# Four pieces of a hybrid decoder layer's schedule are moved: the level 1 update, the third level mask, the relative bias products, the second solution

## The reference

```python
y_s5 = s5_mixer(...)        # z = gelu(y); z * sigmoid(z @ w_glu + b_glu); y from a complex scan over time
y_rw = rwkv7_mixer(...)     # state = state*w + sa*kka + v*k, one step per token
y_mb = moba_mixer(p_mb, rel_bias)   # s = q.k + bias_t[:, t5_bucket(rel)]
y = rms_norm(y.reshape(..., N_GROUPS, GW), mix_out_gain)   # one norm per group
return y.reshape(..., D_MIX) @ w_out
```

## Time and profile before

| | us |
|---|---|
| median of 3 runs | 527.93 |
| lowest and highest | 526.81, 528.66 |
| the profiled execution | 526.82 |
| its span, first to last instruction | 525.0 |
| TensorE busy | 489.0 (93%) |
| VectorE busy | 378.7 (72%) |
| ACT busy | 261.2 (50%) |
| POOL busy | 172.1 (33%) |

### The profile page before, as it was taken

The page is one execution under the profiler, slowest core; times in us unless marked ns, Lnnn a source line. Parts: engine busy times, 40 slices in busy tenths (PEclk is TensorE's granted clock), DMA queues, the critical chain, the costliest instruction groups (busy, mean ns, idle before and its releaser), DMA issues.

```text
span 525.0 us, 8449 instructions
## 1 busy us (share of the span) xinstructions
PE 489.0 (93%) x3478; PEld 447.8 (85%) x3478; DVE 378.7 (72%) x443; ACT 261.2 (50%) x410; POOL 172.1 (33%) x103
## 2 busy tenths in 40 slices
PE   0799999889999999999999995999999999999986
PEld 0789989788898888878999884999999999988874
DVE  5675897997766987679655457589999999962114
ACT  3598774331633244657945547454444443443333
POOL 0030317397669250000000001254433443353440
PEclk9999999989999999999999997899999999999999
DMA  8837328022041023535545241356445555545602
GB/s 345 365 96 248 120 93 308 1 81 81 9 153 53 31 81 116 205 99 223 191 171 201 80 150 40 132 199 236 168 161 168 196 198 180 205 161 196 222 0 81
DMA packets 12358, 79.33 MB, mean 151 GB/s; under 512 B 1440, under 2 KB 2080, under 8 KB 3488
## 3 DMA queue, kind: packets, MB, share of 16 engines
q1 hardware_dynamic: 12320, 78.79, 42.3%
HBM read 76.95 MB, written 1.84 MB: 150 GB/s over the span
## 4 chain that ended last, share of the span: by engine, by line
PE 83%; DVE 9%; ACT 3%; issue 2%; DMA 1%; POOLq 0%; POOL 0%; SPq 0%; DVEq 0%; ACTq 0%
PE bank L369 81%; DMA ring<-weights 1%; DVE arena L1635 1%; DVE vx L1662 1%; ACT w_high L344 1%; DVE arena L1452 1%; PE bank L857 1%; POOLq L89 0%; POOL w_rest L350 0%; DVE arena L1627 0%; DVE we_rest L350 0%; DVE arena L1628 0%; DVE wk_rest L350 0%; DVE arena L1806 0%; DVE wm_rest L350 0%
## 5 line engine op out<-in xcount | busy, mean ns | idle before, releaser
L344 ACT ACTIVATE w_high<-ring 128x1024 fp32r<-128x1024 f32 x70 | 73.6, 1058 | 79.7 <-PE bank L369 79.7
L369 PE MATMUL bank<-h_high,w_high 128*128 128x256 f32 x384 | 103.0, 284 | 0.0
L369 PE MATMUL bank<-h_rest,w_high 128*128 128x256 f32 x352 | 99.7, 283 | 0.0
L369 PE MATMUL bank<-h_high,w_rest 128*128 128x256 f32 x320 | 90.7, 283 | 0.0
L350 DVE TENSOR_TENSOR w_rest<-ring,w_high 128x1024 fp32r<-128x1024 f32 x42 | 53.5, 1279 | 44.2 <-ACT w_high L344 44.1
L350 POOL TENSOR_TENSOR w_rest<-third_slot,w_high 128x1024 fp32r<-128x1024 f32 x11 | 26.5, 2407 | 161.4 <-ACT w_high L344 161.4
L350 POOL TENSOR_TENSOR w_rest<-ring,w_high 128x1024 fp32r<-128x1024 f32 x22 | 53.6, 2438 | 74.8 <-ACT w_high L344 74.8
L369 PEld LDWEIGHTS bank<-h_high,w_high 128*128 128x128 f32 x384 | 71.7, 192 | 0.5 <-issue 0.4
L369 PEld LDWEIGHTS bank<-h_rest,w_high 128*128 128x128 f32 x352 | 67.6, 192 | 0.0
L369 PE MATMUL bank<-arena 128*128 128x128 f32 (+7 forms) x496 | 59.4, 300 | 6.5 <-DVE arena L1658 4.5
L369 PEld LDWEIGHTS bank<-arena 128*128 128x128 f32 (+3 forms) x496 | 52.9, 183 | 12.6 <-DVE arena L1658 5.1
(11 more groups left out here) (308 smaller groups left out, 1227.2 us busy)
## 6 DMA issues: line engine op xcount, KB each, us to landing
ring<-weights SPq DMA_DIRECT2D x50, 1024.0 KB, 4.9
third_slot<-weights SPq DMA_DIRECT2D x15, 1024.0 KB, 4.9
cst<-consts SPq DMA_DIRECT2D x1, 1664.0 KB, 12.3
gain<-gains SPq DMA_DIRECT2D x3, 512.0 KB, 5.9
par<-params SPq DMA_DIRECT2D x1, 1168.0 KB, 14.6
kx<-x_t SPq DMA_DIRECT2D x1, 1024.0 KB, 4.9
vx<-mem_t SPq DMA_DIRECT2D x1, 1024.0 KB, 10.3
xres<-x_rows SPq DMA_DIRECT2D x1, 1024.0 KB, 10.5
```

Source lines behind the costliest of these rows:

```text
L344: nc.scalar.activation(split_half(i)[0], raw_half(i), ACT.Copy).then_inc(S["w_high"], 1)
L369: return nc.tensor.matmul(out_, lhsT, rhs, start=start, stop=stop, skip_group_check=True)
```

## The change

- On TensorE the four bias products stand behind `x_sumsq`, ahead of all projections. They wait for a new semaphore, `onehot_in`; the waits for the large constants and parameters move to the product rw_w.
- The one-hot table moves to the front of the large constants and is loaded by a DMA of its own, 33 partitions of 384, between slots 0 and 1. Only those 33 rows are loaded; before, all 128 were.
- On VectorE, `level_update(1)` and one of the two rests ahead of it stand before `scan(0)`, the other rest between the update and the scan.
- On POOL, `level_mask(3)` stands before `rotate_back(0)`.
- On VectorE, `solution(1)` and one rest stand ahead of the first `sigmoid_of_exp` of S5.
- On TensorE, `gn_s5` stands after step 1 of the output product instead of step 0.

No instruction is added or removed but the one DMA. Some lines of the changed kernel are numbered one to three apart from before.

```diff
--- before.py
+++ after.py
@@ -43,11 +43,10 @@
 
 
 CONST, NCONST = columns([
-    ("ones", P), ("eps6", 1), ("eps12", 1), ("eps_gn", 1), ("eps6_xd", 1), ("round", 1), ("half_pi", 1), ("ident", P), ("pair_ones", P), ("strict", P), ("incl", P), ("causal_add", 384),
+    ("ones", P), ("eps6", 1), ("eps12", 1), ("eps_gn", 1), ("eps6_xd", 1), ("round", 1), ("half_pi", 1), ("onehot", 384), ("ident", P), ("pair_ones", P), ("strict", P), ("incl", P), ("causal_add", 384),
     ("levels", LEVELS * P), ("level0_t", P), ("time", T), ("head_sel", NH * P), ("pair_sel", 2 * P),
-    ("onehot", 384),
 ])
-CONST_FIRST = CONST["ident"][0]
+CONST_FIRST, CONST_MORE = CONST["onehot"]
 
 PARAM, NPARAM = columns([
     ("mu", 8), ("w0", 2), ("a0", 2), ("k_k", 2), ("k_a", 2), ("r_k", 2), ("ln_w", 2), ("ln_b", 2),
@@ -254,7 +253,7 @@
             ml_log ml_cur ml_conv ml_silu ml_E mb_max mb_exp rw_rstd s5_arg s5_exp rw_out s5_out post_sq post_root
             post_part pre_part pre_sq pre_root gain_pre_in x_max f_exp rw_kx rw_G0 rw_k2 s5_co_step
             ml_row_step ml_den mb_inv s5_step2 rw_tail s5_sig x_inv f_sig s5_sq s5_root ml_sq
-            ml_root rw_sq rw_root mb_sq mb_root
+            ml_root rw_sq rw_root mb_sq mb_root onehot_in
             w_high w_rest_even w_rest_odd w_rest_mid w_used high_ready act_rest y_rest h_high h_rest x_summed
             mem_summed
             """.split()}
@@ -566,13 +565,12 @@
             o = pe_open(pe, "x_sumsq", 0)
             pe.wait_ge(S["x_summed"], 4)
             mm(o[:, 0:T], const("ones"), sq_x[:, 0, :]).then_inc(full[0], 1)
-            split_channel_major(0, "rw_wag", 1, h_split, lambda j: pe.wait_ge(S["h_rest"], j + 1))
-            split_channel_major(1, "rw_k", 0, h_split)
-            pe.wait_ge(S["consts_in"], 16)
-            pe.wait_ge(S["params_in"], 16)
+            pe.wait_ge(S["onehot_in"], 16)
             for h in range(NH):
                 o = pe_open(pe, f"rel{h}", 4 + h)
                 mm(o[:, 0:384], prm("rel", 33)[:, h:h + 1].to_broadcast([33, P]), const("onehot", 33)).then_inc(full[4 + h], 1)
+            split_channel_major(0, "rw_wag", 1, h_split, lambda j: pe.wait_ge(S["h_rest"], j + 1))
+            split_channel_major(1, "rw_k", 0, h_split)
             split_channel_major(2, "rw_r", 1, h_split)
             o = pe_open(pe, "mem_sumsq", 7)
             pe.wait_ge(S["mem_summed"], 3)
@@ -581,6 +579,8 @@
             split_channel_major(4, "s5_u", 1, h_split)
 
             o = v3(pe_open(pe, "rw_w", 2)[:, :], T)
+            pe.wait_ge(S["consts_in"], 16)
+            pe.wait_ge(S["params_in"], 16)
             pe.wait_ge(S["rw_low"], 1)
             for j in range(2):
                 last = mm(o[:, j, :], prm("w2a2")[0:HD, j * P:(j + 1) * P], rwE[0:HD, 0, 0, :])
@@ -778,7 +778,7 @@
                     pe.wait_ge(S["y_rest"], kt // 2 + 1)
 
             def group_sums(kt):
-                if kt == 0:
+                if kt == 1:
                     group_sumsq("gn_s5", 0, 3)
                 if kt == 3:
                     group_sumsq("gn_rw", 2, 6)
@@ -916,8 +916,10 @@
             sp.dma_start(cst[:, 0:CONST_FIRST], consts_d[:, 0:CONST_FIRST]).then_inc(S["first_in"], 16)
             sp.dma_start(par[:, 0:PARAM_FIRST], params_d[:, 0:PARAM_FIRST]).then_inc(S["first_in"], 16)
             for n in range(NSLOTS):
+                if n == 1:
+                    sp.dma_start(cst[0:33, CONST_FIRST:CONST_MORE], consts_d[0:33, CONST_FIRST:CONST_MORE]).then_inc(S["onehot_in"], 16)
                 if n == 2:
-                    sp.dma_start(cst[:, CONST_FIRST:], consts_d[:, CONST_FIRST:]).then_inc(S["consts_in"], 16)
+                    sp.dma_start(cst[:, CONST_MORE:], consts_d[:, CONST_MORE:]).then_inc(S["consts_in"], 16)
                     sp.dma_start(par[:, PARAM_FIRST:], params_d[:, PARAM_FIRST:]).then_inc(S["params_in"], 16)
                 if n == 3:
                     sp.dma_start(mem_h, v3(mem_t, NMEM)).then_inc(S["mem_in"], 16)
@@ -1023,8 +1025,8 @@
             rotate(0)
             level_mask(1)
             level_mask(2)
+            level_mask(3)
             rotate_back(0)
-            level_mask(3)
             rotate(1)
             rotate_back(1)
             level_mask(4)
@@ -1663,9 +1665,10 @@
                                               ALU.mult, ALU.mult)
             last.then_inc(S["mem_ready"], 1)
 
+            rests(H_MID + 3)
+            level_update(1)
+            rests(H_MID + 4)
             scan(0)
-            rests(H_MID + 4)
-            level_update(1)
 
             dve.wait_ge(S["ml_log"], 3)
             moved(dve, "gates")
@@ -1811,12 +1814,12 @@
             rests(H_WKV + 9)
             solve_rhs(1)
             rests(H_WKV + 10)
+            solution(1)
+            rests(H_WKV + 11)
             dve.wait_ge(S["s5_exp"], 1)
             sigmoid_of_exp(z5b, "s5_sig", 0).then_inc(S["s5_sig"], 1)
             dve.wait_ge(S["s5_sig"], 2)
             v.tensor_tensor(z5, z5y, z5b, ALU.mult).then_inc(S["s5_z"], 1)
-            rests(H_WKV + 11)
-            solution(1)
             group_gain(1, "ml")
             rests(H_WKV + 12)
             rests(H_LATE + 2)
```

## The result

| | before | changed |
|---|---|---|
| median, us | 527.55 (10 runs) | 524.66 (10 runs) |
| lowest and highest, us | 526.63, 528.66 | 524.29, 526.5 |
| the profiled execution, us | 526.82 | 526.5 |
| its span, us | 525.0 | 524.7 |

The changed kernel takes 0.9949 of the time before, 95% interval 0.9939 to 0.9959: 2.9 us or 0.5% less. The forecast was 6.7 us less. The changed kernel's profiled execution is the slowest of its ten; the other nine lie between 524.3 and 525.1. So its trace shows more loss than the median has, and one place of it (118 to 131 us) has to be read beside other kernels' traces.

What follows compares the result with a forecast made beforehand. TensorE was taken as the bound (83% of the span), so only its idle or slow-clock time could be won. Terms 1.0 + 3.6 + 1.3 + 0.8 = 6.7 us off 527.93 gave 521.3 us, range 519.2 to 525.2.

Steps and rivals of the forecast that it cites:

- cases that keep 2.7 us: Whole kernel: mixed cases keeping about 2.7 us of the gain, which set the range's slow end at 525.2.
- Part 1: Kernel start: relative bias products moved into TensorE's idle gap after x_sumsq, 1.0 us won (-0.5 to 1.5).
- half 8: Half slot on TensorE for S5's input: its rest ready at 44.0, two halves from there ending at 49.8.
- ACT's stream: Start: ACT works without a gap from 23.09 to 50.0, so most of TensorE's own 5.0 us is not kept.
- Part 2: Levels: level 1's update ahead of the scans on VectorE, 5.6 us won, 3.6 kept (2.2 to 4.4).
- The 5.6 us at mb_k: TensorE after levels 1 and 2: 3.97 us of idle and 1.7 us of slow clock gone.
- the fall at 107: Level 2's products on TensorE: granted clock of 0.50 at 107 to 108 costs 1.7 us, forecast to go.
- Parts 3 and 4: Late in the kernel: second solution first, 1.3 us (0.8 to 1.3); S5 group sum after step 1, 0.8 (0 to 0.8).
- POOL is stopped more often: Levels: VectorE's two-input instructions stop POOL pieces, scan 1 at 125.8, 2.2 us kept there; 522.7, chance 0.25.
- the second rival: Start: TensorE's clock falls in the idle before mem_sumsq, or bias input lands late; gives 0 to -0.5; 522.5, chance 0.15.

Runs made afterwards that it cites:

- bias_full_rows: Changed kernel with the relative bias products over all 128 rows in place of 33, added rows zero: 524.63 us, ratio 0.9953.
- part 2 alone: Kernel before with only the level update ahead of the scans and third mask ahead of first rotate back, two runs: 529.22, ratio 1.0021; 528.83, ratio 1.0011.
- other_bank: Changed kernel with S5's projection in bank 3 in place of 1, and rw_a in 1 in place of 3: 524.18 us, ratio 0.9943.
- scan_first_silu: Changed kernel with slot 0's scans before level_update(1), third mask behind first rotate back, silu product behind level 2's update: 521.91 us, ratio 0.9902.
- combined kernel: Changed kernel with scans first, third mask behind rotate back, silu product late, S5's projection in bank 3: 520.96 us, ratio 0.988.
- levels_only: Kernel before with only the level update ahead of the scans and the third mask ahead of the first rotate back: 529.22 us, ratio 1.0021.
- levels_full_rows: Kernel before with only the level part, and the bias products in their old place over 128 rows in place of 33: 526.92 us, ratio 0.9998.

## Why the prediction was wrong

The direction was right, the range (519.2 to 525.2) held the time, and the size was off by more than half: 2.9 us for 6.7. Two of four terms failed. That the range held is no credit to the mechanism: it reached down to cases that keep 2.7 us, worked out for other reasons.

- **Part 1, 1.0 us: measured 0.0 (trace 0.2).** Two steps of it failed. "The clock, which rose after 5.2 us of work begun at 16.42, should be up by then" is wrong: work of 33 rows did not raise it, work of 128 rows did. And half 8 was put at 44.0, when its rest is ready; it also needs bank 1, which the mix of slot 2 gives up at 44.7. With that bank exchanged the trace has 0.3 us more, not 0.7. That the DMA would be in time, and that ACT's stream would swallow most, was right.
- **Part 2, 3.6 of 5.6 kept: measured between plus 1.0 and minus 2.3 in the traces, nothing or a loss on its own.** The 5.6 us at mb_k are there. The step that failed is what gives them back, in three places.
  - Level 2's update was to free bank 4 at 117.1; it did at 118.7. Of these 1.6 us, 1.3 are the scans: they were forecast to end at 107.3 and ended at 108.6, since the third mask ran beside them.
  - POOL was forecast to be ready for scan 1 at 123.7; the scan began at 125.94. Rotate back began 1.3 us later than forecast, and its pieces and rotate's were hindered by 4.4 us, not 3.7 (6.02 and 10.97 us for ten pieces of 1.26). Rotate back was forecast to end at 112.5, ahead of the readout; it ended at 114.7, and TensorE waited 0.94 us for it.
  - The fourth mask was late by that, and then slow. In bias_full_rows, whose clock held, VectorE's next work (h_rest, L1485) ran beside it:

```profile
133.69 4.10 POOL L1019 TENSOR_TENSOR arena<-arena,cst 128x512 f32<-128x512 f32 x2
```
```profile
133.55 3.29 DVE L1485 TENSOR_TENSOR h_rest<-vx,h_high 128x1024 fp32r<-128x1024 f32 x2
```
```profile
135.86 1.13 PE L368 MATMUL bank<-arena 128*128 128x128 f32 x8 [0.21 <-issue]
137.89 1.13 PE L368 MATMUL bank<-arena 128*128 128x128 f32 x8 [0.90 <-issue]
```

  The mask's two halves end at about 135.7 and 137.8, and level 4's two halves start there. It began 2.2 us later than before the change (131.46) and took 4.10 us in place of 2.15. Had it taken 2.15, its halves would have been ready at about 134.8 and 135.8, before TensorE wanted them (an estimate from these rows). In the changed kernel's own trace, where TensorE was later and h_rest too, the mask took 2.15 us. Less the start's 0.11 us, the lead was 2.65 us at level 3, 2.35 at level 3's second products and 0.96 behind level 4. The forecast had 4.4 at level 3, gave 0.8 away at level 4 and ended with 3.6.
- **The clock in the level part was no term at all.** It was counted as a gain (1.7 us, the fall at 107 gone) and in part 1 as a risk, not as something that the new waits of part 2 bring back. They did, in the same size or larger, in all but one of the profiled executions that have part 2 as it stands in the change.
- **Parts 3 and 4, 1.3 and 0.8: right.** 1.34 and 0.8 in the traces, 2.5 us measured for the pair. Nothing took them back, and the reciprocal's and the gain's later ends stayed covered.
- **The rivals.** "POOL is stopped more often" named scan 1 at 125.8 (measured 125.94) and the fourth mask as the place, but its mechanism is only a part: POOL is late first because it waits for scans that start 4.5 us later, then because of hindrance. That its 125.8 came so close is in part luck: it had 5.8 us of hindrance where 4.4 were measured, and rotate back on time. Its 522.7 was still 2 us too low: 1.0 of that is part 1, which it left at its full value, and it had neither the later update of level 2 nor the clock. That part 1 gives nothing was the second rival. Its time came true, its mechanism did not: TensorE waited 0.80 us before mem_sumsq and the clock held; only bias_full_rows shows the fall that it meant. Part 1 at nothing, a dearer part 2 and the clock's price in it came together, where the prediction took the rivals as alternatives.

The parts measured alone do not add up to the whole: 0.0 for part 1, 0.6 to 1.1 us lost for part 2 (ratios 1.0011 and 1.0021) and 2.5 won make 1.4 to 1.9, and the change measures 2.7 by the same count (2.9 by the medians). In the changed kernel none of ten executions had a mean clock of 0.98 or less, with part 2 alone 12 of 21. The bias products' new place doesn't settle it: other_bank and bias_full_rows have that place too, with 1 such execution of 6 and 4 of 11. Why stays open.

Three sums of the prediction are slightly off, without effect on the account: 117.1 against 121.69 leaves 4.6 us, not 4.4; the first subtraction begins at 105.62, not 105.70; and 527.93 less 6.7 is 521.2.

## What to carry to other kernels

When a step is moved ahead on one engine to spare TensorE a wait, follow what is moved behind it to the engine that waits for that, through the whole chain. Here four scans stood ahead of VectorE's next update and fed a chain on POOL whose end, 30 us later, TensorE came to wait for; putting the scans first with the update right behind them kept both early. Price a wait of TensorE that the new order leaves twice, once as idle time and once as half pace behind it, and expect the second only in some executions. Look also at what the engine beside it now runs at the same time: a mask of 2.15 us took 4.10. And measure the parts of a bundle apart: two small moves late in this kernel measured about as much alone as the whole.

## What the runs showed of the hardware that was not expected

- Matmuls of few rows did not raise TensorE's clock: after 5.49 us of products over 33 of 128 rows the next 19 matmuls still took 0.21 us each; after 3.99 us of the same products over 128 rows, and 2.08 us of waiting, they took 0.12. The first holds in twelve profiled kernels (13 to 28 slow matmuls), the second in the one that had it.
- The clock can fall without a wait of note: in scan_first_silu TensorE waited 0.38 us before level 3 and then had products of 4 rows, and ran at 0.50 from 122 to 125 us. In the profiled execution of the combined kernel, with the same 0.38 us, it held. Behind one and the same wait of 1.93 us it held (bias_full_rows), fell for some 3 us (levels_only) or for some 10 (changed, other_bank, levels_full_rows). Executions of one kernel differ by 4 us and more (525.0 to 529.6 in levels_full_rows, at mean clocks of 0.991 and 0.98).
- Matmuls whose result is thrown away, set into waits of 2.4 and 4.0 us, kept the clock at 1.00 and made the kernel 1.7 us faster by the medians (520.96 and 519.29, in different turns; the intervals of the two ratios lie apart).
- Two of VectorE's scans took 1.5 us beside a POOL mask and 0.66 alone. The Trainium skill, "SBUF — State Buffer", section "Who interferes with whom", says that a VectorE instruction with two SBUF inputs contends with a GpSimd instruction that reads SBUF. The rows here agree and show both sides lose: two scans took 0.9 us longer each, and the two masks 3.27 in place of 2.15 us.
